# Scores two turns ahead placed first in a turn's TensorE order, in a float32 transformer kernel for one Trainium2 core

## The chip, the cores and the metric

The kernel runs on one NeuronCore of one Trainium2 chip. The metric is the device time of one execution in microseconds (us); lower is better. Every time below is of this core. A profile is one execution of the same program taken by the hardware profiler.

## What is computed

Two transformer blocks over 512 tokens of width 1024, all in float32: a block with two gated feed-forward layers, a spatial gating mixer and a pooling mixer, and a second block with a short convolution, sparse attention and dilated attention. The change touches the sparse attention of the second block alone. Its selected-blocks branch and its window branch cover all causal keys at this length (512 tokens, at most 16 blocks of 64, window 512), so both are plain causal attention with keys and values of their own:

```python
s_s = jnp.einsum("bqgrd,bqgkld->bqgrkl", qb, k_sel) * scale
p_s, _, _ = _masked_softmax(s_s, m_s)
o_s = jnp.einsum("bqgrk,bqgkd->bqgrd", p_s, v_sel)
...
s_w = jnp.einsum("bqgrd,bkgd->bqgrk", qb, kw) * scale
p_w, _, _ = _masked_softmax(s_w, m_w)
o_w = jnp.einsum("bqgrk,bkgd->bqgrd", p_w, vw)
return gb[..., 0:1] * o_c + gb[..., 1:2] * o_s + gb[..., 2:3] * o_w
```

There are six query heads in two key/value groups of three; `o_c` is a third branch over 31 compressed keys.

## The kernel before, in words

**Engines and order.** Each engine has its instruction list written out by hand; nothing is scheduled by a tool. TensorE's list is the function `tensor`, ScalarE's is `scalar`, VectorE's is `vector`. The engines wait for each other by named semaphores (`pe.wait_ge(signal, key)`), and each engine executes its own list strictly as written.

**Main work.** Nearly all of TensorE's time goes to projections: each float32 product is made of three products of split halves (`xh*whi`, `xh*wlo`, `xl*whi`), 512 columns each, accumulated in the PSUM banks `G`. For each weight block a DMA brings `raw`, ScalarE makes the high half `whi` (L64), VectorE the low half `wlo` (L70).

**Background work.** The attention of the second block is a Python generator, `attention()`, that is advanced ("pumped") from the loop over the 21 column tiles of the second block's input projection. A tile is 24 matmuls of 512 columns, and after every six of them `pump(background)` issues the next piece. All three engines hold such a generator with matching `yield`s, so a piece stands at the same place of each list.

**The sparse attention.** Its work is 24 pairs: three heads per group (`r_`), four query blocks (`i`), two branches (`b`). Pairs are grouped in 18 *turns*, six for each `r_`: pairs (0, 1), (2, 3), (4,), (5,), (6,), (7,). Both groups (`j` or `g` = 0 and 1) are done together, in partitions 0 to 63 and 64 to 127. For a turn `v` there are these pieces:

- `scores(v)`: TensorE multiplies queries and keys (`kvn`, `qn`), 64 rows deep, into bank `X[0]` (j = 0) and `X[1]` (j = 1). These banks are single: the first product of turn `v` in bank `j` waits for `nm_done` of turn `v-1`, group `j`, the masking pass of the turn before.
- VectorE's `score(n)`: one pass (L82, `prb<-X,mcaus`) reads the scores from the bank, adds the mask, writes `prb` and takes the row maximum into `stat`; an accumulator read (also L82) ends it and raises `nm_done`. ScalarE then takes the exponential in place, with its sum.
- VectorE's `scale(v)`: a reciprocal (L85) and the multiplications by it and the gate (L76).
- `turn_sp(v)`: TensorE transposes `prb` into `X[2]` (j = 0) and `G[2]` (j = 1); ScalarE copies the first to `ptr` (L64), VectorE the second (L67).
- `weigh(v)`: the value products, `vnt` by `ptr`, and for the first branch of each query block also `vcs` by `sq_t` (the compressed branch), accumulated in `X[3]` or `G[3]`; the last raises `o_done`.

**The order around the change.** A step `u` of the loop in TensorE's `sparse()` issues three pieces, in this order: the value products of turn `u-1`, the scores of turn `u+2`, the transposes of turn `u`. Two pumps are between steps (12 matmuls of 512 columns), three after the first and last step of each `r_`. VectorE's step `u`, in its own list, is: copy of turn `u`'s transposes (L67), `scale(u+1)`, `score` of turn `u+2`; between steps it does pieces of the projections (`wlo`, and evictions such as `nz<-G`, `cab<-G`, `cac<-G`). So the scores of turn `u+2` in TensorE's step `u` wait for the masks of turn `u+1`, which VectorE does at the end of its step `u-1`. After the last turn of an `r_`, VectorE's `weigh` multiplies the finished output with `nz` (L70, `tmp_t<-X,nz`) once `o_done` is raised, before the next copy.

The wait that guards a score bank is in `score`:

```python
elif c0 == 0 and n > DIL and o == 0:
    pe.wait_ge(nm_done, (TURNS[turn_no[n] - 1][-1], j))
```

Where the text says V, it means VectorE; "ready" is the moment from which a waiting TensorE instruction starts.

Of the kernel before, what the change touches and what calls it, by code (L numbers as in the profile page):

```python
# [120 lines left out]
def two_blocks(nc, A, out):  # L121
    ctx = ExitStack()
    with ctx:
# [357 lines left out]
        TURNS = [[DIL + 8 * r_ + p for p in turn] for r_ in range(3) for turn in ((0, 1), (2, 3), (4,), (5,), (6,), (7,))]  # L481
# [4 lines left out]
        def blocks(n):  # L486

            if n >= DIL:
                return pairs_sp[n - DIL][1] + 1
            i, gi = pairs_dil[n]  # L490
            return 2 if i and gi == 0 else 1

        def place(n):

            o = sum(blocks(before) for before in turn_of[n] if before < n) * 128
            return slice(o, o + blocks(n) * 128)
# [26 lines left out]
        def prob(n, j):  # L523
            if n < DIL:
                s = 2 * (DIL_TURNS.index(turn_of[n]) % 4) + j
                return (prb[:, s, :] if s < 4 else tmps[s - 4])[:, place(n)]
            return prb[:, 2 * (turn_no[n] % 2) + j, place(n)]

        def copied(n, j):

            return (pt_dve, (n, 1)) if j else (pt_act, (n, 0))
# [59 lines left out]
        def tensor(pe):  # L591
# [320 lines left out]
            def score(n, i, k0, q, k):  # L912

                nk = (i + 1) * 128 - k0
                o = place(n).start
                for c0 in range(0, nk, 256):
                    c1 = min(c0 + 256, nk)
                    for j in range(2):
                        if c0 == 0 and n == 0:
                            pe.wait_ge(rooted, "s4")  # L920
                            pe.wait_ge(rpre_done, "s4")
                        elif c0 == 0 and n > DIL and o == 0:
                            pe.wait_ge(nm_done, (TURNS[turn_no[n] - 1][-1], j))
                        elif c0 == 0 and n == DIL:
                            pe.wait_ge(mixed, ("cmp", j))
                        elif c0 == 0 and n < DIL and o == 0:
                            pe.wait_ge(nm_done, (n - 1, j))
                        t = pe.matmul(X[j][:, o + c0:o + c1], q[64 * j:64 * j + 64, i * 128:(i + 1) * 128],
                                      k[64 * j:64 * j + 64, k0 + c0:k0 + c1], True, True)
                        if c1 == nk and n == turn_of[n][-1]:  # L930
                            t.then_inc(*score_done.event((n, j)))
# [129 lines left out]
            def sparse():  # L1061
                def scores(u):
                    for n in TURNS[u]:
                        r_, i, b = pairs_sp[n - DIL]
                        pe.wait_ge(stored, ("q", r_))
                        pe.wait_ge(stored, ("kv", 2 + b))
                        score(n, i, 0, qn[:, r_, :], kvn[:, 2 + b, :])

                def turn_sp(u):
                    for j in range(2):  # L1070
                        if u % 6 == 0:
                            pe.wait_ge(pt_act, ("c", u // 6, j))
                        else:
                            pe.wait_ge(*copied(TURNS[u - 1][-1], j))
                        for n in TURNS[u]:
                            pe.wait_ge(p_scaled, (n, j))
                            to = (G[2] if j else X[2])[:, place(n)]
                            for b in range(blocks(n)):
                                t = pe.transpose(to[:, b * 128:(b + 1) * 128], prob(n, j)[:, b * 128:(b + 1) * 128], ident[:, :])
                        t.then_inc(*p_turned.event((TURNS[u][-1], j)))  # L1080

                def coarse(r_):
                    pe.wait_ge(p_scaled, "cmp")
                    for g in range(2):
                        if r_:
                            pe.wait_ge(*((pt_dve, (DIL + 8 * r_ - 1, 1)) if g else (pt_act, (DIL + 8 * r_ - 1, 0))))
                        for i in range(4):
                            t = pe.transpose((G[2] if g else X[2])[0:31, i * 128:(i + 1) * 128],
                                             pcmp[:, i * 6 + g * 3 + r_, 0:31], ident[:, :])
                        t.then_inc(*p_turned.event(("c", r_, g)))  # L1090

                def weigh(u):
                    for n in TURNS[u]:
                        weigh_pair(n, TURNS[u][-1])

                def weigh_pair(n, last):
                    r_, i, b = pairs_sp[n - DIL]
                    bank = G[3] if r_ % 2 else X[3]
                    o = [bank[64 * g:64 * g + 64, i * 128:(i + 1) * 128] for g in range(2)]
                    if b == 0:  # L1100
                        if i == 0:
                            pe.wait_ge(*((od_done, 2) if r_ == 1 else (od_done, 0) if r_ == 0 else (mixed, ("ob", 0))))
                        pe.wait_ge(mixed, "vcs")
                        for g in range(2):
                            pe.wait_ge(pt_act, ("c", r_, g))
                            pe.matmul(o[g], vcs[:, 64 * g:64 * g + 64], sq_t[:, g, i * 128:(i + 1) * 128], True, False)
                    pe.wait_ge(*copied(last, 0))
                    pe.wait_ge(*copied(last, 1))
                    for k in range(i + 1):
                        c = place(n).start + k * 128  # L1110
                        for g in range(2):
                            t = pe.matmul(o[g], vnt[:, k, 128 * b + 64 * g:128 * b + 64 * g + 64],
                                          ptr[:, g, c:c + 128], False, b == 1 and k == i)
                    if n == last:
                        t.then_inc(*o_done.event(n))

                scores(0)
                yield
                scores(1)
                yield  # L1120
                coarse(0)
                yield
                for u in range(len(TURNS)):
                    if u:
                        weigh(u - 1)
                    if u + 2 < len(TURNS):
                        scores(u + 2)
                    turn_sp(u)
                    yield
                    if u + 1 < len(TURNS) and (u + 1) % 6 == 0:  # L1130
                        coarse((u + 1) // 6)
                    yield
                    if u % 6 in (0, 5):
                        yield
                weigh(len(TURNS) - 1)

            def attention():
                yield from dilated()
                yield from compress()
                yield from sparse()  # L1140
# [1888 lines left out]
```

## Time and profile before

| | |
|---|---|
| time, median of 3 runs | 1520.35 us (1519.77 to 1520.39) |
| the profiled execution's own time | 1519.88 us |
| its span in the trace | 1517.8 us |
| TensorE matmuls | 1508.3 us, 99% of the span, 7596 instructions |
| TensorE weight loads | 1249.0 us, 82% |
| VectorE | 891.4 us, 59% |
| ScalarE | 626.9 us, 41% |
| GpSimd | 134.0 us, 9% |
| DMA | 162.99 MB, 107 GB/s over the span |
| granted TensorE clock | 0.999 of full speed |
| the sparse attention's turns | about 1283 to 1401 us of the span |

The profile lists instructions with start and duration. Matmul records overlap, since matmuls are pipelined: a record of 0.39 us may be followed by the next one 0.227 us later. So TensorE's pace is read from start to start, and a busy share of 99% does not exclude a short wait hidden under the record before it.

### The profile page before, as it was taken

The page shows a single profiled execution, that of the slowest core. Times are in us where ns is not written, and L with a number is a line of the kernel's source. Part 1 is how long each engine was busy: PE and PEld are TensorE (multiplying, and loading weights), DVE is VectorE, ACT ScalarE, POOL GpSimd, SP SyncE. Part 2 cuts the span into 40 slices and gives each one's busy share as a digit, 9 for nine tenths or more (in the row PEclk, how much of TensorE's full clock was granted, in tenths as well). Part 3 has the DMA queues.
Part 4 walks back from the last instruction along what each step waited for, and adds up shares of the span by engine and source line. Part 5 has one row for each costly group of instructions (what it writes and reads, how often), then busy time and mean ns, then how long its engine had stood idle before and what let it go on. Part 6 is the DMA issues. An engine that isn't in the chain of part 4 may idle for free.

```text
span 1517.8 us, 18953 instructions
## 1 busy us (share of the span) xinstructions
PE 1508.3 (99%) x7596; PEld 1249.0 (82%) x7596; DVE 891.4 (59%) x1420; ACT 626.9 (41%) x980; POOL 134.0 (9%) x147
## 2 busy tenths in 40 slices
PE   9999999999999999999999999999999999999998
PEld 7888888888888888888888888888888887777886
DVE  6556765557545633344865576565648465667645
ACT  6343333337433323233734333333556442544345
POOL 2101000001012500001100101000000020001100
PEclk9999999999999999999999999999999999999999
DMA  5556365432322322333245646443232472211322
GB/s 182 125 141 170 110 162 124 112 107 88 94 87 84 97 83 84 97 97 111 84 111 139 144 124 152 121 113 111 83 97 81 110 151 57 57 43 55 125 84 96
DMA packets 132856, 162.99 MB, mean 107 GB/s; under 512 B 19385, under 2 KB 87169, under 8 KB 132769
## 3 DMA queue, kind: packets, MB, share of 16 engines
q1 hardware_dynamic: 122080, 138.56, 30.8%
q0 software_dynamic: 10688, 23.22, 8.5%
q8 instruction: 60, 0.98, 0.3%
q14 instruction: 28, 0.22, 0.0%
HBM read 159.11 MB, written 2.65 MB: 107 GB/s over the span
## 4 chain that ended last, share of the span: by engine, by line
PE 97%; ACT 1%; DVE 1%; DMA 0%; issue 0%; POOL 0%; POOLq 0%; ACTq 0%
PE G L58 78%; PE X L58 16%; PE X L61 2%; PE G L61 1%; ACT sq_t L64 0%; DMA raw<-in_w_in_dram 0%; ACT whi L64 0%; ACT xh L64 0%; DVE prb L76 0%; ACT prb L64 0%; ACT f L64 0%; DVE xl L73 0%; DVE h L73 0%; ACT post L64 0%; DVE f L70 0%
## 5 line engine op out<-in xcount | busy, mean ns | idle before, releaser
L70 DVE TENSOR_TENSOR wlo<-raw,whi 128x1024 fp32r<-128x1024 f32 (+3 forms) x245 | 294.9, 1207 | 344.5 <-ACT whi L64 344.3
L58 PE MATMUL G<-xh,whi 128*128 128x512 f32 (+1 forms) x1168 | 454.8, 391 | 0.2 <-ACT whi L64 0.2
L58 PE MATMUL G<-xl,whi 128*128 128x512 f32 (+1 forms) x1168 | 449.9, 387 | 0.4 <-DVE xl L73 0.4
L58 PE MATMUL G<-xh,wlo 128*128 128x512 f32 (+1 forms) x1168 | 449.5, 386 | 0.3 <-issue 0.3
L64 ACT ACTIVATE whi<-raw 128x1024 fp32r<-128x1024 f32 (+3 forms) x245 | 251.7, 1031 | 402.1 <-DMA raw<-in_ffn_w_up_dram 185.6
L58 PEld LDWEIGHTS G<-xl,whi 128*128 128x128 f32 x1168 | 219.3, 188 | 46.0 <-DVE xl L73 0.8
L58 PEld LDWEIGHTS G<-xh,whi 128*128 128x128 f32 x1168 | 219.2, 188 | 44.5 <-issue 0.8
L58 PEld LDWEIGHTS G<-xh,wlo 128*128 128x128 f32 x1168 | 219.5, 188 | 42.9 <-DVE wlo L70 0.4
L58 PE MATMUL G<-whi,xh 128*128 128x512 f32 (+2 forms) x256 | 96.9, 379 | 0.0
L58 PE MATMUL G<-whi,xl 128*128 128x512 f32 (+2 forms) x256 | 95.1, 372 | 0.2 <-DVE xl L73 0.2
L58 PE MATMUL G<-wlo,xh 128*128 128x512 f32 (+2 forms) x256 | 94.7, 370 | 0.0
L58 PE MATMUL X<-whi,mixh 128*128 128x512 f32 x224 | 87.1, 389 | 0.0
L58 PE MATMUL X<-wlo,mixh 128*128 128x512 f32 x224 | 87.1, 389 | 0.0
L58 PE MATMUL X<-whi,mixl 128*128 128x512 f32 x224 | 87.1, 389 | 0.0
L64 ACT ACTIVATE act_t<-act_t 128x512 f32<-128x512 f32 x70 | 44.0, 632 | 89.4 <-DVE act_t L70 89.4
L70 DVE TENSOR_TENSOR wlo<-chain,whi 128x1024 fp32r<-128x1024 f32 x32 | 39.1, 1222 | 52.5 <-ACT whi L64 52.5
L103 POOL DMA_DIRECT2D chain<-in_ffn_w_down_dram x24 | 28.9, 1202 | 418.2 <-DVE wlo L70 418.2
L64 ACT ACTIVATE whi<-chain 128x1024 fp32r<-128x1024 f32 x32 | 33.7, 1053 | 71.0 <-DMA chain<-in_ffn_w_down_dram 71.0
L70 DVE TENSOR_TENSOR f<-f,X 128x512 f32<-128x512 f32 x96 | 61.3, 680 | 0.0
L70 DVE TENSOR_TENSOR act_t<-G,rpre 128x512 f32<-128x512 f32 x68 | 46.4, 686 | 17.4 <-PE G L58 17.1
L58 PEld LDWEIGHTS G<-whi,xl 128*128 128x128 f32 x256 | 48.1, 188 | 8.6 <-DVE xl L73 0.8
L58 PEld LDWEIGHTS G<-whi,xh 128*128 128x128 f32 x256 | 48.1, 188 | 8.3 <-issue 0.9
(304 smaller groups left out, 2093.8 us busy)
## 6 DMA issues: line engine op xcount, KB each, us to landing
raw<-in_w_in_dram SPq DMA_DIRECT2D x55, 512.0 KB, 3.7
raw<-in_ffn_w_gate_dram SPq DMA_DIRECT2D x88, 256.0 KB, 2.9
raw<-in_ffn_w_up_dram SPq DMA_DIRECT2D x88, 256.0 KB, 3.1
raw<-in_ffn_w_down_dram SPq DMA_DIRECT2D x28, 512.0 KB, 3.7
chain<-in_ffn_w_down_dram POOLq DMA_DIRECT2D x24, 512.0 KB, 5.9
raw<-in_w_in_dram SPq DMA_DIRECT2D x12, 384.0 KB, 3.2
chain<-in_ffn_w_down_dram SPq DMA_DIRECT2D x8, 512.0 KB, 4.9
pair_sum<-in_ffn_w_down_dram SPq DMA_DIRECT2D x8, 512.0 KB, 4.8
```

The source lines that it names most:

```text
L58: return self.e.matmul(out, lhs, rhs, start=start, stop=stop, skip_group_check=onto) if self.e else Idle()
L61: return self.e.transpose(*a) if self.e else Idle()
L64: return self.e.activation(*a, **kw) if self.e else Idle()
L70: return self.e.tensor_tensor(*a) if self.e else Idle()
L103: return self.e.dma_start(out, src, accum_op=ALU.add) if self.e else Idle()
```

## The change

In TensorE's step `u` of the sparse attention the scores of turn `u+2` are issued before the value products of turn `u-1`; the transposes of turn `u` stay last. Every wait and every operation is the same, and no other engine's list is touched.

```diff
                 for u in range(len(TURNS)):
+                    if u + 2 < len(TURNS):
+                        scores(u + 2)
                     if u:
                         weigh(u - 1)
-                    if u + 2 < len(TURNS):
-                        scores(u + 2)
                     turn_sp(u)
                     yield
```

TensorE's list in step 8 (value products of turn 7, scores of turn 10, transposes of turn 8), between two projection matmuls, before the change (`kvn,qn` are scores, `sq_t,vcs` and `ptr,vnt` value products, `ident,prb` transposes):

```order
L58 MATMUL G<-xl,whi 128x512
L58 MATMUL G<-sq_t,vcs 64x128 x2
L58 MATMUL G<-ptr,vnt 64x128 x8
L58 MATMUL X<-kvn,qn 128x256 x4
L61 MATMUL X<-ident,prb 128x128 x3
L61 MATMUL G<-ident,prb 128x128 x3
L58 MATMUL G<-xh,whi 128x512
```

and in the changed kernel:

```order
L58 MATMUL G<-xl,whi 128x512
L58 MATMUL X<-kvn,qn 128x256 x4
L58 MATMUL G<-sq_t,vcs 64x128 x2
L58 MATMUL G<-ptr,vnt 64x128 x8
L61 MATMUL X<-ident,prb 128x128 x3
L61 MATMUL G<-ident,prb 128x128 x3
L58 MATMUL G<-xh,whi 128x512
```

The four score matmuls moved ahead of ten value products. This is so in steps 1 to 15. Step 0 has no value products and steps 16 and 17 no scores, so they stay as they were. The other four engines' lists are the same, line for line. TensorE's list in step 13 (value products of turn 12, scores of turn 15, transposes of turn 13), before the change:

```order
L58 MATMUL X<-sq_t,vcs 64x128 x2
L58 MATMUL X<-ptr,vnt 64x128 x4
L58 MATMUL X<-kvn,qn 128x256 x2
L58 MATMUL X<-kvn,qn 128x128 x2
L61 MATMUL X<-ident,prb 128x128 x4
L61 MATMUL G<-ident,prb 128x128 x4
```

and in the changed kernel:

```order
L58 MATMUL X<-kvn,qn 128x256 x2
L58 MATMUL X<-kvn,qn 128x128 x2
L58 MATMUL X<-sq_t,vcs 64x128 x2
L58 MATMUL X<-ptr,vnt 64x128 x4
L61 MATMUL X<-ident,prb 128x128 x4
L61 MATMUL G<-ident,prb 128x128 x4
```

Here four score matmuls (384 columns in each of the two groups' banks) moved ahead of six value products.

## Rows read from the trace of the kernel before

**Rows 1.** The page: busy time of TensorE, and the chain that ended last.
```profile
PE 1508.3 (99%) x7596; PEld 1249.0 (82%) x7596; DVE 891.4 (59%) x1420; ACT 626.9 (41%) x980; POOL 134.0 (9%) x147
...
PE 97%; ACT 1%; DVE 1%; DMA 0%; issue 0%; POOL 0%; POOLq 0%; ACTq 0%
```

**Rows 2.** Timeline, TensorE, step 7: start us, busy us, engine, line, operation, out<-in.
```profile
1333.16 0.39 PE L58 MATMUL G<-xh,wlo 128*128 128x512 f32 x1
1333.39 0.39 PE L58 MATMUL G<-xl,whi 128*128 128x512 f32 x1
1333.71 0.44 PE L58 MATMUL G<-sq_t,vcs 128*64 128x128 f32 x4
1333.98 0.61 PE L58 MATMUL G<-ptr,vnt 128*64 128x128 f32 x8
1334.52 0.92 PE L58 MATMUL X<-kvn,qn 64*128 64x256 f32 x8
1335.37 0.66 PE L61 MATMUL X<-ident,prb 128*128 128x128 f32 x4
...
1336.22 0.48 PE L58 MATMUL G<-xh,whi 128*128 128x512 f32 x1
```

**Rows 3.** Timeline, TensorE, step 13; in brackets the idle time before, and its releaser.
```profile
1370.80 0.44 PE L58 MATMUL X<-sq_t,vcs 128*64 128x128 f32 x4
...
1371.89 1.40 PE L58 MATMUL X<-kvn,qn 64*128 64x256 f32 x8 [0.21 <-DVE stat L82]
1373.21 0.66 PE L61 MATMUL X<-ident,prb 128*128 128x128 f32 x4
```

**Rows 4.** Timeline, VectorE: accumulator reads that end turn 14's masks (j = 0, 1).
```profile
1371.75 0.08 DVE L82 DVE_READ_ACCUMULATOR2_ANT stat<- 128x1 f32 x1
...
1372.23 0.08 DVE L82 DVE_READ_ACCUMULATOR2_ANT stat<- 128x1 f32 x1
```

**Rows 5.** Timeline, TensorE: step 0, scores after projections; step 16, transposes after value products.
```profile
1290.22 0.40 PE L58 MATMUL G<-xl,whi 128*128 128x512 f32 x1
1290.55 0.92 PE L58 MATMUL X<-kvn,qn 64*128 64x256 f32 x8
...
1388.49 0.88 PE L58 MATMUL X<-ptr,vnt 128*64 128x128 f32 x12
1389.30 0.66 PE L61 MATMUL X<-ident,prb 128*128 128x128 f32 x4
```

**Rows 6.** Timeline, TensorE: where the value products of step 8 begin.
```profile
1339.14 0.44 PE L58 MATMUL G<-sq_t,vcs 128*64 128x128 f32 x4
```

**Rows 7.** Timeline, VectorE: from the masks of turn 8 to those of turn 9.
```profile
1328.27 0.69 DVE L70 TENSOR_TENSOR tmp_t<-X,nz 128x512 f32<-128x512 f32 x1 [1.53 <-PE X L58]
...
1333.06 0.08 DVE L82 DVE_READ_ACCUMULATOR2_ANT stat<- 128x1 f32 x1
1334.99 1.23 DVE L70 TENSOR_TENSOR wlo<-raw,whi 128x1024 fp32r<-128x1024 f32 x1 [1.84 <-ACT whi L64]
...
1337.33 0.68 DVE L67 COPY ptr<-G 128x512 f32<-128x512 f32 x1
...
1339.86 0.08 DVE L82 DVE_READ_ACCUMULATOR2_ANT stat<- 128x1 f32 x1
```

**Rows 8.** Timeline, VectorE: copies of turns 8 and 9, last accumulator read of turn 10.
```profile
1342.93 0.55 DVE L67 COPY ptr<-G 128x384 f32<-128x384 f32 x1
...
1345.59 0.09 DVE L82 DVE_READ_ACCUMULATOR2_ANT stat<- 128x1 f32 x1
...
1347.99 0.56 DVE L67 COPY ptr<-G 128x384 f32<-128x384 f32 x1 [1.71 <-PE G L61]
```

**Rows 9.** Timeline, ScalarE: the high half that follows turn 8's exponentials.
```profile
1333.91 1.04 ACT L64 ACTIVATE whi<-raw 128x1024 fp32r<-128x1024 f32 x1
```

**Rows 10.** Waits of VectorE in 1283 to 1401: waiter <- releaser: us, times, longest.
```profile
DVE wlo L70 <- ACT whi L64: 15.3, 10, 2.0
DVE ptr L67 <- PE G L61: 10.4, 10, 2.6
```

## The prediction, as it was put on record before the changed kernel ran

> **What bounds the kernel.** The page comes first. TensorE is busy 99% of the span and makes 97% of the chain that ended last [rows 1], so any time added to TensorE's list in the attention ends up in the total, and the list holds no large wait that a new order could remove. What is left is to ask whether TensorE waits longer or shorter in the 15 turns whose order changes. For that I read the timeline of TensorE from start to start. Two projection matmuls are 0.227 us apart (1333.16, 1333.39 [rows 2]); that is the pace. In step 7 a turn costs the same as its neighbours of the same shape: value products begin at 1333.71, scores 0.81 later at 1334.52, transposes 0.85 later at 1335.37, projections again at 1336.22 [rows 2]. Step 13 has the same shape of value products and a scores piece of the same width, but goes differently: value products at 1370.80, so the scores could start at 1371.61; they start at 1371.89, and the transposes come not 0.85 later but at 1373.21 [rows 3]. The trace puts 0.21 us of idle time beside it; the real loss is 1373.21 - (1371.61 + 0.85) = 0.75 us, the rest hidden under overlapping records. The cause is VectorE's masks of turn 14: the reads that end them start at 1371.75 and 1372.23 and last 0.08 [rows 4]. The first score matmul starts 0.06 after the first read's end, and the transposes come at 1372.23 + 0.14 + 0.85. So a piece of scores is **ready** 0.14 after the start of the second read, and its whole length follows from there. In the other 14 turns the value products, ahead of the scores, cover the masks. That cover is what the change takes away.
>
> **The change, part by part.** It adds and removes no instruction. In steps 1 to 15 the scores move ahead by the length of the value products, 0.8 to 1.2 us.
>
> *Switches between shapes.* The pieces use the array in three shapes: 128 by 128, 128 rows by 64 columns, 64 rows by 128 columns. Projection to value products takes 0.32 in place of 0.227 [rows 2]; projection to scores 0.33 [rows 5]; from the last value product (1333.98 + 0.61 - 0.27, a last record being 0.27 long) to the scores 0.20, from the scores to the transposes 0.20 [rows 2]; from value products to transposes 0.20 (1388.49 + 0.88 - 0.27, 1389.30 [rows 5]), where such small matmuls or pairs of them are 0.11 apart. So each switch costs about 0.09, and there are three of them per turn before and after. One of the new three, scores to value products, stands in no row. I take the 0.09 of the others: sum 0, plus 0.01 a turn for the 0.33 against 0.32, 0.1 in all. Its bounds: nothing (15 x -0.09 = -1.4 us) and twice as much (+1.4). The Trainium skill, TensorEngine Tiling, Key Properties, says that changing the tiling mode drains the array, whichever modes they are; by that the sum of the switches is 0, and the two bounds would fall away.
>
> *Waits of the scores.* Now turn by turn. "Begins" is where the value products begin before the change, which is where the scores would begin after it. "Ready" is the second read's start of turn u+1's masks plus 0.14. D is by how much VectorE is late against before when it ends those masks, S by how much TensorE is late after the step. The added wait is ready + D - begins - S of the step before, if positive. The starts of steps 7, 8 and 13, and the masks for step 9, stand in [rows 2 to 4], [rows 6 to 8]; the others are the same two kinds of record, of their turns, in the same timelines.
>
> | step u | begins | ready | D | added wait | S |
> |---|---|---|---|---|---|
> | 1 | 1296.62 | 1295.56 | 0 | 0 | 0 |
> | 2 | 1302.05 | 1302.08 | 0 | 0.03 | 0.03 |
> | 3 | 1307.90 | 1308.08 | 0.03 | 0.18 | 0.21 |
> | 4 | 1313.56 | 1314.03 | 0.03 | 0.29 | 0.50 |
> | 5 | 1318.80 | 1318.84 | 0.50 | 0.04 | 0.54 |
> | 6 | 1327.13 | 1325.59 | 0.54 | 0 | 0.54 |
> | 7 | 1333.71 | 1333.20 | 1.40 | 0.35 | 0.89 |
> | 8 | 1339.14 | 1340.00 | 1.40 | 1.37 | 2.26 |
> | 9 | 1344.99 | 1345.73 | 1.69 | 0.17 | 2.43 |
> | 10 | 1350.65 | 1350.94 | 2.43 | 0.29 | 2.72 |
> | 11 | 1355.89 | 1356.64 | 2.43 | 0.46 | 3.18 |
> | 12 | 1364.22 | 1362.69 | 3.18 | 0 | 3.18 |
> | 13 | 1370.80 | 1372.37 | 3.18 | 1.57 - 0.75 | 4.00 |
> | 14 | 1376.98 | 1377.96 | 3.18 | 0.16 | 4.16 |
> | 15 | 1382.83 | 1383.01 | 4.16 | 0.18 | 4.34 |
>
> D is the part that needs care, for VectorE is late only if what it waited for is late. Its chain to the masks begins with the copy of transposes. Where VectorE stood idle for them, as at 1347.99 with 1.71 idle, released by TensorE [rows 8], D becomes S. The transposes can be copied 0.28 after the projections start again; so at the copy of turn 7 (1337.33, possible from 1336.22 + 0.28 = 1336.50 [rows 2, 7]) VectorE was 0.83 behind, and S must exceed that before it counts. Such margins stand at the copies of turns 3 (0.19), 7 (0.83), 8 (0.57), 10 (0.71), 13 (0.95); elsewhere it waited. Where the copy is not reached by S, D is carried on by the chain that made VectorE late: masks of turn 8, exponentials, the high half at 1333.91 [rows 9], the low half `wlo` at 1334.99 after 1.84 idle waiting for it, then evictions and the copy [rows 7]. That chain has no TensorE in it. The jump to 1.40 is in step 6. VectorE's product `tmp_t` at 1328.27 waited 1.53 for the last value product of turn 5 [rows 7], and that now stands behind 0.86 us of scores: 0.54 + 0.86. At the same place in step 12 VectorE came 2.1 late to it, so nothing is added there.
>
> What is queued behind a waiting score: the value products and transposes of the step and 12 to 18 projections; VectorE's and ScalarE's copies then come later, and this is in D. The weight halves `wlo` come later by D, which exceeds S by at most 0.86; no wait on them stands in this stretch. The DMAs are issued by queues that the change leaves alone. After 1401 TensorE has no wait that could swallow a delay: its pace stays 0.227 up to the end, so S is paid in full.
>
> **Sum.** 4.34 + 0.1 = 4.4 us. The profiled execution took 1519.88, so it would take 1524.3; against the median, 1520.35 + 4.4 = **1524.8 us**, 0.29% slower. Differences within 0.2% (3 us) are about what a measurement of this kernel cannot tell from none.
>
> **Rivals.**
> 1. *VectorE keeps its own times* (D = 0 all along). Then a first wait shifts TensorE once, and the next masks find it late already: S grows only to the largest excess, 0.86 at step 8, and ends at 1.0. Time 1521.3, within 0.2%. For it: VectorE's idle times before `wlo`, 15.3 us in the attention, are put down to ScalarE [rows 10]. Against: ten copies waited for transposes (10.4 us [rows 10]), and the exponentials that precede `whi` wait for the masks themselves. It decides if the copies of turns 9 and 11 do not move with TensorE.
> 2. *Every delay is carried whole* (no margin absorbs anything): the waits are 0.03, 0.18, 0.47, 0.04, 0.35, 1.37, 0.74, 0.29, 0.75, 0.82, 0.98, 0.18, sum 6.2 us: 1526.6. For it: VectorE's list has more work in a turn (copy, scale, masks, a low half) than the pauses after it show. Against: the margins above.
> 3. *The work behind the waiting scores runs on.* If value products, whose operands are long there, could pass scores that wait, nothing would be lost: 1520.4. Against it: in step 13 the transposes, scaled long before, did not pass [rows 3]. The Trainium skill, TensorE: Matmul & The Clock Gate, What happens when you issue a matmul, says that matmuls stay in program order and only weight loads are pulled ahead; the trace agrees (1373.21), and this rule is what speaks against the change.
> 4. *The unseen switch is free*, with the waits as forecast: 1523.4, at the edge.
>
> **How the numbers follow.** The forecast 0.65, rival 2 0.13, rival 1 0.12, rival 4 0.07, rival 3 0.03. To be faster by 3 us no mechanism is in sight: only one wait of 0.2 (ScalarE, step 0) and the 0.75 stand in the whole stretch; 0.02 for surprise. Within 0.2%: rivals 1 and 3 and a part of 4, 0.18. Slower by more: 0.80. The range takes in rival 2 with a little of the switch's upper bound, and below the forecast less the switch and some of the carrying: 1522.0 to 1527.2.
>
> **What would show it.** In the profile of the changed kernel TensorE's scores wait for `stat` (VectorE, L82), most of all in steps 8 and 13, where the piece from the last projection to the first next one should take about 4.6 in place of 3.26 and 4.4 in place of 3.58. Step 12 and step 6 keep their lengths. Scores to value products should show 0.20 from last to first start. In VectorE's timeline the copy of turn 9 should come 2.4 us later than before. The prediction is wrong if the waits are there but the last value products of the attention come less than 3 us later, or if the turns without waits change their length by more than 0.1.

## The result, and the profile after

The changed kernel takes 1524.41 us (median of 8 runs, 1524.15 to 1525.41) where the kernel before takes 1520.32 (8 runs, 1519.77 to 1521.23): the ratio is 1.0028, with a 95% interval of 1.0020 to 1.0037. Predicted were 1524.8 us and 0.29%.

The page of the changed kernel, busy times and the chain that ended last:

```profile
span 1522.8 us, 18953 instructions
...
PE 1511.5 (99%) x7596; PEld 1251.8 (82%) x7596; DVE 891.7 (59%) x1420; ACT 627.2 (41%) x980; POOL 133.9 (9%) x147
...
PE 94%; ACT 2%; DVE 2%; DMA 1%; issue 0%; POOL 0%; POOLq 0%; ACTq 0%; DVEq 0%
```

Instruction counts are those of [rows 1] and TensorE still shows 99%: the busy share says nothing of what happened. The chain says a little: 97% on TensorE became 94%, and ScalarE and VectorE have 2% each in place of 1% each. The span grew by 5.0 us, of which 0.67 lies ahead of the attention, where the two programs are the same (the last projection matmul before the first scores starts at 1283.77 in place of 1283.10, and over the profiles of all kernels here between 1282.67 and 1283.91). So from here on I compare one stretch: from that matmul to the first projection matmul after the last value products. It was 117.38 us and is 121.70, which is 4.33 more; with the 0.67 ahead of it that is the whole growth of the span.

The timeline of TensorE in step 8, as [rows 6] begins it (start us, busy us; in brackets the idle time before and its releaser):

```profile
1340.39 0.39 PE L58 MATMUL G<-xl,whi 128*128 128x512 f32 x1
1341.60 1.61 PE L58 MATMUL X<-kvn,qn 64*128 64x256 f32 x8 [0.82 <-DVE stat L82]
1343.14 0.44 PE L58 MATMUL G<-sq_t,vcs 128*64 128x128 f32 x4
...
1345.01 0.47 PE L58 MATMUL G<-xh,whi 128*128 128x512 f32 x1
```

and of VectorE, the two accumulator reads that end turn 9's masks, then the copies of turns 8 and 9:

```profile
1341.46 0.08 DVE L82 DVE_READ_ACCUMULATOR2_ANT stat<- 128x1 f32 x1
...
1341.94 0.09 DVE L82 DVE_READ_ACCUMULATOR2_ANT stat<- 128x1 f32 x1
...
1345.29 0.56 DVE L67 COPY ptr<-G 128x384 f32<-128x384 f32 x1 [0.20 <-PE G L61]
...
1351.10 0.56 DVE L67 COPY ptr<-G 128x384 f32<-128x384 f32 x1 [2.45 <-PE G L61]
```

Scores that wait for nothing start 0.33 after the last projection matmul [rows 5], here at 1340.39 + 0.33 = 1340.72. They start at 1341.60, 0.06 after the first read ends, and the value products behind them, whose operands were there (the later of turn 7's two copies ended on VectorE at 1340.09), start 1.20 after the start of the second read (0.14 and 1.06; before the change this piece of step 8, four times 256 columns for each group, took 1.06 without a wait). From the last projection matmul to the first next one it is 4.62 us; before it was 3.26. Step 13 shows the same, with more in brackets than the 0.21 of [rows 3]:

```profile
1375.73 1.39 PE L58 MATMUL X<-kvn,qn 64*128 64x256 f32 x8 [1.01 <-DVE stat L82]
1377.06 0.44 PE L58 MATMUL X<-sq_t,vcs 128*64 128x128 f32 x4
```

The added length of each step, from last projection matmul to first next one, against the prediction's table:

| step | predicted | measured | step | predicted | measured |
|---|---|---|---|---|---|
| 1 | 0 | 0.00 | 9 | 0.17 | 0.14 |
| 2 | 0.03 | 0.03 | 10 | 0.29 | 0.31 |
| 3 | 0.18 | 0.17 | 11 | 0.46 | 0.46 |
| 4 | 0.29 | 0.29 | 12 | 0 | 0.00 |
| 5 | 0.04 | 0.04 | 13 | 0.82 | 0.80 |
| 6 | 0 | 0.00 | 14 | 0.16 | 0.15 |
| 7 | 0.35 | 0.34 | 15 | 0.18 | 0.15 |
| 8 | 1.37 | 1.36 | sum | 4.34 | 4.25 |

The other 0.08 of the 4.33 us stand in step 0 (0.01) and in the projections between the steps (0.07). The view of waits in this stretch counts less than half of the 4.25:

```profile
PE X L58 <- DVE stat L82: 2.0, 3, 1.0
```

It sees three waits, of steps 8, 11 and 13, and of these only what sticks out behind the record before. After the attention neither kernel has a wait of TensorE in the view of waits, so nothing gave the loss back.

### The profile page after: what moved, and what is told of

Its sections match the earlier page's. It is cut to its first block, busy times and chain, and to the rows that moved or that the text cites. A ratio compares the mean times of both kernels' runs of the same rounds, so it can differ in the third digit from the quotient of the medians.

```text
span 1522.8 us, 18953 instructions
## 1 busy us (share of the span) xinstructions
PE 1511.5 (99%) x7596; PEld 1251.8 (82%) x7596; DVE 891.7 (59%) x1420; ACT 627.2 (41%) x980; POOL 133.9 (9%) x147
## 4 chain that ended last, share of the span: by engine, by line
PE 94%; ACT 2%; DVE 2%; DMA 1%; issue 0%; POOL 0%; POOLq 0%; ACTq 0%; DVEq 0%
PE G L58 76%; PE X L58 15%; PE X L61 2%; ACT prb L64 1%; DVE prb L76 1%; PE G L61 1%; ACT sq_t L64 0%; ACT whi L64 0%; DMA stat<-stat_rows 0%; DVE wlo L70 0%; DMA stat_rows<-stat 0%; ACT tmp_t L64 0%; DVE prb L82 0%; DMA raw<-in_w_in_dram 0%; DVE ptr L67 0%
```

## The experiments

All lengths are of the stretch, from one profile each; the kernel before has 117.38, the changed one 121.70. One profile each is enough for lengths of steps: those that a run's edit and its waits leave alone repeat to 0.001 us in nearly every profile. Totals are medians, beside that of the kernel before, measured together with it.

**1. The new order in step 8 alone.**

```diff
                 for u in range(len(TURNS)):
+                    if u in (8,):
+                        scores(u + 2)
                     if u:
                         weigh(u - 1)
-                    if u + 2 < len(TURNS):
+                    if u + 2 < len(TURNS) and u not in (8,):
                         scores(u + 2)
```

> The scores go ahead of the value products in step 8 alone. Theory (the value products covered VectorE's masks; the cost is the wait for them): step 8 takes 0.86 us longer (masks ready 1340.00, scores would begin 1339.14), no other step changes its length, and the stretch from the last projection matmul before the first scores to the first one after the last value products grows from 117.38 to 118.24 us. Rival (the new order itself, such as the switch between array shapes, costs about 0.29 us in each of 15 turns): 117.7. Rival (waits add up, 1.37 belongs to step 8 by itself): 118.75.

Measured: step 8 takes 4.105 in place of 3.256, 0.85 more; no other of the steps 1 to 17 changes by more than 0.001; the stretch is 118.28. In total 1521.03 beside 1519.84, ratio 1.0007 (0.9998 to 1.0017), too little to be told from none. So the same swap costs 0.85 here and 1.36 in the changed kernel: the other 0.51 was brought from elsewhere.

**2. The new order in steps 1, 6 and 12 alone** (the same edit, with `(1, 6, 12)`).

> The scores go first only in steps 1, 6 and 12, where the masks they need were ready long before. Theory: these three steps keep their lengths within 0.02 us each; but in step 6 the last value product of turn 5 now ends 0.86 later, VectorE's product with nz waits for it, and the lateness reaches steps 8 and 9, whose own order is as before: they grow by 0.48 and 0.10, the stretch by 0.6 to 117.97. Rival (the order itself costs 0.29 a turn): the three steps grow, 8 and 9 do not, 118.25. Rival (only the wait in a swapped step matters): 117.38.

Measured: 1520.51, ratio 1.0004 (0.9994 to 1.0013). Steps 1, 6 and 12 take 2.827, 2.608 and 2.609: unchanged. Step 8, whose order is the old one, takes 3.709 (0.45 more) and step 9 3.139 (0.10 more); the stretch is 117.94. The carrier is seen in VectorE's product of step 6 (1.53 of idle time before it in [rows 7]) and in the end of turn 9's masks; then TensorE's step 8:

```profile
1329.28 0.69 DVE L70 TENSOR_TENSOR tmp_t<-X,nz 128x512 f32<-128x512 f32 x1 [2.39 <-PE X L58]
...
1340.86 0.08 DVE L82 DVE_READ_ACCUMULATOR2_ANT stat<- 128x1 f32 x1
```

```profile
1340.54 1.59 PE L58 MATMUL X<-kvn,qn 64*128 64x256 f32 x8
1342.06 0.55 PE L61 MATMUL X<-ident,prb 128*128 128x128 f32 x3
```

The scores piece is 1.52 from its start to the transposes where 1.06 is its length. The row has no bracket: group 0 starts in time, group 1 waits, and the record beside it hides that. The swap made no matmul of TensorE wait where it was made and cost 0.55 us two and three steps later. This also settles the switch between scores and value products that no row of before showed: three swapped steps keep their length to 0.001 us, so the three switches of the new order cost in sum what those of the old one do.

**3. The change, undone in steps 8 and 13**, which hold 2.16 of the 4.25 us (this edit is shown against the changed kernel).

```diff
-                    if u + 2 < len(TURNS):
+                    if u + 2 < len(TURNS) and u not in (8, 13):
                         scores(u + 2)
                     if u:
                         weigh(u - 1)
+                    if u in (8, 13):
+                        scores(u + 2)
                     turn_sp(u)
```

> The change, undone in steps 8 and 13, where the two largest waits stand (added 1.36 and 0.80 of 4.33 us). Theory (a wait makes TensorE late and so pays for the waits after it): walking the steps as in the prediction, step 8 grows by 0.13, step 9 by 1.12, step 10 by 0.29, step 11 by 0.46, step 13 by 0, step 14 by 0.98, step 15 by 0.18, and the stretch is 121.5, only 0.2 less than with the change. Rival (waits belong to their steps and add up): 121.70 - 2.16 = 119.5.

Measured: 1523.76 beside 1519.84, ratio 1.0024 (1.0015 to 1.0034). Steps 8 and 13 grow by 0.12 and 0.00, but step 9 by 1.13 (with the change 0.14) and step 14 by 0.97 (0.15); the stretch is 121.35. Step 9 now looks like step 8 above:

```profile
1346.23 1.74 PE L58 MATMUL X<-kvn,qn 64*128 64x256 f32 x8 [0.45 <-DVE stat L82]
1347.90 0.44 PE L58 MATMUL G<-sq_t,vcs 128*64 128x128 f32 x4
```

Taking away half of the waits' time got back 0.35 us. A wait is not a price of its step: what bounds these steps is when VectorE is done with its masks, and a TensorE that did not wait in step 8 comes too early in step 9.

**4. Value products, transposes, scores**, in every step.

```diff
                     if u:
                         weigh(u - 1)
+                    turn_sp(u)
                     if u + 2 < len(TURNS):
                         scores(u + 2)
-                    turn_sp(u)
                     yield
```

> In every step value products, transposes, scores: the scores last, so that the masks are covered by both. Theory: no wait of scores for masks anywhere (the 0.75 us of step 13 goes), but a turn has four switches of array shape in place of three, at 0.09 us each, in 15 steps: 117.38 - 0.75 + 1.35 = 118.0. If switches cost nothing or are only paid towards scores: 116.6. If the cost of the change was the place of the scores before the transposes and not a wait: slower than 119.

Measured: 1522.97 beside 1519.84, ratio 1.0020 (1.0011 to 1.0029), stretch 120.62. No scores wait, step 13 takes 3.00 in place of 3.58, as expected. The sum was wrong at two places. Step 0 takes 3.13 in place of 2.11, because its transposes wait for ScalarE's `sq_t`, a wait that the scores of turn 2 mostly covered before (0.19 was left by the view, 0.26 from start to start):

```profile
1290.21 0.40 PE L58 MATMUL G<-xl,whi 128*128 128x512 f32 x1
1291.63 0.44 PE L61 MATMUL X<-ident,prb 128*128 128x128 f32 x2 [1.03 <-ACT sq_t L64]
```

And each of the other 14 steps up to 15 is 0.17 longer, not 0.09. The additional switch is the one from the scores back to the projections: the first projection matmul starts 0.20 after a last score of 128 columns, where it started 0.03 after the last transpose (projections and transposes use the array in the same shape). And a switch costs more than the gap at it: the first interval behind it is longer too. Here the first two projection matmuls are 0.34 apart in place of 0.31, 0.02 more in each of the 15 steps, so that the switch costs 0.20 in all. With 1.01 for step 0 and 15 x 0.174 for the switches, less 0.75, the stretch comes to 120.25; the other 0.37 are in just these first intervals. The total is over the 119 that the expectation names for its rival, the place of the scores before the transposes. But here the scores stand behind the transposes, none of them waits, and the terms above fill the difference, so this run does not speak for it.

**5 and 6. Less work on VectorE between copy and masks**, under the old and under the new order. Most of the scaling is left out, so the output of both is wrong; they serve for timing alone.

```diff
-                            dve.tensor_scalar(p, p, den_of(n, g), gates[:, i, o:o + 1], ALU.mult,
+                            dve.tensor_scalar(p[:, 0:32], p[:, 0:32], den_of(n, g), gates[:, i, o:o + 1], ALU.mult,
                                               ALU.mult).then_inc(*p_scaled.event((n, g)))
```

> The order of before; VectorE multiplies only the first 32 columns of each block of probabilities by the reciprocal and the gate (the others are left unscaled), so its work between a copy and the masks is 0.3 to 0.6 us shorter per turn. Theory: the masks of turn 14 are ready in time, the 0.75 us of step 13 goes: stretch 116.6.

> The changed order with the same part left out on VectorE. Theory (VectorE's lateness is the cost): waits are left in step 8 (about 0.7) and step 13 (about 0.7) alone, stretch about 118.2, 1.5 over the same cut with the old order, where the uncut pair differs by 4.33. Rival (the order itself): the pair still differs by about 4.3.

Measured, with one time each (1519.73 and 1521.68, beside 1520.41): the old order has 116.74, step 13 takes 2.91, so 0.08 of its wait is left; the new order has 118.38, with 0.87 added in step 8 and 0.80 in step 13 (2.91 to 3.72), nothing in the other 13. The pair differs by 1.64 us where the full pair differs by 4.33. TensorE's two lists are those of the full pair; shortening VectorE took 2.7 us off the price of the order. In step 8 of the new order:

```profile
1340.35 1.61 PE L58 MATMUL X<-kvn,qn 64*128 64x256 f32 x8 [0.32 <-DVE stat L82]
1341.88 0.44 PE L58 MATMUL G<-sq_t,vcs 128*64 128x128 f32 x4
```

**7. Transposes, value products, scores**, in every step (`turn_sp(u)` moved to the head of the step).

> In every step transposes, value products, scores: three switches of array shape as before (projections and transposes share one), scores last. Theory: no scores wait for masks; in place of the 0.75 us of step 13 the transposes of steps 13 and 14 wait for their scaling, about 0.25 each: stretch 117.0, 0.4 less than before. Rival: transposes so early wait in most steps, over 118.

Measured: 1521.04 beside 1520.41, ratio 1.0006 (0.9997 to 1.0015), stretch 118.70. With three switches the steps are 0.03 longer than before, step 8 is 0.14 longer, step 13 is 0.72 shorter and step 14 has no wait; but step 0 pays the same 1.01 for `sq_t` as in run 4, which I had again left out. Without it the stretch would be 117.7, which is still not the 117.0 of the expectation: the 0.03 in each step come to 0.5, and 0.46 more are in the projections between the steps, most of it in their first intervals behind the scores, as in run 4. That the stretch is over 118 fits the number of the expectation's rival but not its mechanism: beside step 0 only step 8 (0.11 over the 0.03) shows more than the price of the new order.

**8. Value products, transposes, scores in steps 13 and 14 only.**

```diff
                     if u:
                         weigh(u - 1)
+                    if u in (13, 14):
+                        turn_sp(u)
                     if u + 2 < len(TURNS):
                         scores(u + 2)
-                    turn_sp(u)
+                    if u not in (13, 14):
+                        turn_sp(u)
```

> The order of before, but in steps 13 and 14 the transposes go ahead of the scores. Theory: step 13 loses its 0.75 us wait and pays one more switch (0.09), step 14 pays one more switch and its scores still find the masks ready: 117.38 - 0.57 = 116.8, which in the total is 0.04% and not measurable there. Changed in step 13 alone, step 14 would wait 0.40 of it back.

Measured: 1519.88 beside 1520.41, ratio 0.9997 (0.9988 to 1.0006), stretch 117.04. Step 13:

```profile
1372.34 0.66 PE L61 MATMUL X<-ident,prb 128*128 128x128 f32 x4
...
1373.37 0.92 PE L58 MATMUL X<-kvn,qn 64*128 64x256 f32 x8
1374.22 0.50 PE L58 MATMUL G<-xh,whi 128*128 128x512 f32 x1
```

The scores are 0.85 long, without a wait. Steps 13 and 14 change by -0.57 and +0.17, the latter the fourth switch at its real price. With 0.09 more in the projections and 0.02 less in step 0, the stretch is 0.33 us shorter than before (0.57 was expected), the shortest with the whole computation, and the total can't be told from that of before.

**9. Transposes, value products, scores in steps 13 and 14 only** (the edit of run 8, with `turn_sp(u)` ahead of `weigh(u - 1)`).

> The order of before, but in steps 13 and 14 transposes, value products, scores. From the run with this order in every step: step 13 takes 2.86 (before 3.58) and step 14 3.28 (3.26), the other steps stay as before; stretch 117.38 - 0.72 + 0.03 = 116.7, the shortest of all with the whole computation, but 0.05% of the total and not measurable there. Rival (step 14 waits for masks or scaling that came no earlier, as a late VectorE would make it): step 14 3.5 or more, stretch 117.0.

Measured: 1520.09 beside 1520.27, ratio 0.9999 (0.9990 to 1.0008), stretch 117.36. Step 13 takes 2.96, but step 14 takes 3.80 in place of 3.26: the rival. Its transposes come before VectorE has scaled them (the second block is VectorE's scaling):

```profile
1375.64 0.39 PE L58 MATMUL G<-xl,whi 128*128 128x512 f32 x1
1376.29 0.52 PE L61 MATMUL X<-ident,prb 128*128 128x128 f32 x3 [0.26 <-DVE prb L76]
```

```profile
1375.66 0.87 DVE L76 TENSOR_SCALAR prb<-prb,stat,gates 128x384 f32<-128x384 f32 x2
```

In run 7 TensorE reached this place 2.6 us later (1378.27) and VectorE began that scaling only 1.5 later (1377.14 against 1375.66), so it was ready there, and the step lengths of run 7 could not be carried over to a kernel in which TensorE is early. This is run 3 once more, from the other side.

## Why the prediction was right

**What bounds the kernel.** That added TensorE time is paid in full held: 4.33 us more in the stretch, 4.1 in the medians, and no wait later on. Reading starts and not idle times was needed: the waits view shows 2.0 us.

**Switches.** Zero in sum within the steps, where the prediction had 0.1 (0.01 a turn). Run 2 shows it for the switch that was not in the trace, and in the changed kernel steps 1, 6 and 12 keep their length. So rival 4, the free switch, is out, and so are both bounds. That the 0.08 us outside of the 15 steps come near to the 0.1 is chance. The rule of the Trainium skill (TensorEngine Tiling, Key Properties, a change of mode drains the array) agrees with this: the switch from scores to value products takes 0.20 after a scores piece that ends with 128 columns, like the others. But the 0.09 that I gave for the price of one switch was too small; runs 4 and 8 have 0.17 for an additional one in its step, and run 4 another 0.02 behind it. It cancelled because the number of switches stayed the same.

**Waits.** The table of the prediction holds in every step to 0.03 us. Its column D is met to 0.03 us at the second read of every turn from 2 to 16. It can be read at VectorE's copies too: the copy of turn 8 at 1345.29 is 2.36 later than in [rows 8], less the 0.67 of the start 1.69, as predicted; the copy of turn 9, which waited before, comes 2.44 later by the same count, where 2.43 was S; `tmp_t` of step 6 comes 1.41 later for 1.40. One reading was incomplete without harm: the prediction lets VectorE wait at all copies but five, yet in the trace of before it comes late to those of turns 6, 12 and 15 as well (by 0.57, 2.64 and 0.19, counted as there). In steps 6 and 12 D was already as large as S, and after step 15 no scores follow.

**The rivals.** VectorE keeping its own times is out: its copies of turns 9 and 11, on which the prediction let this rival hang, came 2.44 and 3.18 later, each after a wait for TensorE, and the loss is 4.3 and not 1.0. Every delay carried whole is out: step 9 added 0.14 and not 0.74, step 14 0.15 and not 0.98; the margins absorbed the rest. Value products running past the waiting scores is out by step 8: they start only behind them. The order as such costing something is out by runs 2 and 6.

**What stays open.** The largest waits stand in steps 8 and 13, and in step 13 the kernel before already loses 0.75 us. Which of VectorE's other work (evictions, convolution) makes its masks late there, and what it would bring to move it, was not tried. Under the old order it is an estimate that this brings under 1 us: run 5 got back 0.63 and run 8 0.33.

## What to carry to other kernels

A piece of work that stands ahead of a waiting instruction is its cover; before moving it, write down for each turn when the awaited result is ready and when the moved instruction would arrive, with the lateness of both engines carried along, since carrying every delay whole (6.2 us here) and not carrying VectorE's at all (1.0) were both wrong. An order that delays nothing where it stands can delay another engine's input and be paid several steps later (run 2), and removing one wait of an engine that follows a slower one mostly moves it to the next step (runs 3 and 9). A wait that the profile shows as 0.2 us may be 0.75: measure a step from start to start against one of the same shape.

## What the runs showed that I had not expected

- An additional change of array shape in a step costs 0.17 us in the step and 0.02 behind it (run 4), about twice the 0.09 by which the gap at a switch exceeds the pace (0.20 where 0.11 is the pace). The first interval within the new shape is longer as well: with a switch ahead of them the first two transposes are 0.166 apart where later ones are 0.110, while in run 7, where projections stand ahead of them and the shape stays, it is 0.107.
- TensorE's waits for the second group's masks leave no bracket at all when the first group's matmul runs beside them (run 2, step 8: 0.45 us, no idle time shown).
